# Taking the experts of a mixture in turn, those with two slots and those with one: places ranked on VectorE, each section's weights found by SyncE in a table

## The chip, the cores and the metric

One Trainium2 chip, one of its cores. The metric is the device time of one execution in microseconds (us); for several executions the median is given. The profile and the trace come from one profiled execution, and its times are counted from the span's start.

## The reference

The trunk has two layers over 512 frames of 1024 columns, all in float32. Each layer is a mixer block (two attentions, gated and merged) and then a feed-forward block, which is dense in layer 0 and a mixture of 8 experts in layer 1. The change concerns the mixture alone:

```python
logits = (h @ w_router).astype(jnp.float32)
top_v, top_i = lax.top_k(logits, TOP_K)          # TOP_K = 2 of N_EXPERTS = 8
top_w = jax.nn.softmax(top_v, axis=-1)
combine = jnp.sum(jax.nn.one_hot(top_i, N_EXPERTS) * top_w[..., None], axis=-2)
out = jnp.zeros_like(h)
for e in range(N_EXPERTS):                       # D_FF_EXPERT = 1408
    out = out + combine[..., e:e + 1] * swiglu(h, w_gate[e], w_up[e], w_down[e])
```

512 frames with two experts each make 1024 pairs, 128 per expert on the average. The sum over the experts does not depend on their order.

## The kernel before

The kernel is written engine by engine, with semaphores by hand; each engine's function is a list of instructions in the order in which it runs them. It has no scheduler. Every float32 product is made of three matmuls of rounded halves (high by high, low by high, high by low), for which ScalarE writes the high half of each weight unit and VectorE the low half.

**Routing.** TensorE computes the router's logits and turns them so that frames lie on partitions. VectorE finds the two largest per frame with small operations on 32 columns, and writes picks. TensorE multiplies picks by a triangle and by ones, which gives each frame's rank within its expert (columns 0 to 31 of bank 3) and the number of frames of each expert (columns 64 to 71). From the ranks VectorE works out a column and a row of the lists for each of the 1024 entries (spot, lines 1061 to 1076), writes them as one-hot tiles (in_column, entry_hit, row_hit, lines 1078 to 1085), and TensorE sums these into lists, which hold for each slot of each expert the frames to fetch and the rows to store to. Nearly each of these operations is wrapped in link(), which makes VectorE wait until it is done. The twice_e tile, written by POOL, is twice the expert's number and so the column of its first slot: place and expert are the same.

**Sections.** Then eight sections follow, one per expert, in a hardware loop on each engine (passes on TensorE, VectorE and ScalarE; weights on SyncE; moves on POOL, unrolled). A slot is a block of up to 128 frames of one expert. An expert with at most 128 frames has one slot; one with more has a second, called the tail, of 64 rows. On TensorE, VectorE and ScalarE the body stands twice, for two slots and for one, and each section reads its count from counts and branches (If counts[i] > 128). With the reference's inputs experts 0, 1, 6 and 7 have more than 128 frames and experts 2, 3, 4 and 5 have not, so the sections come as two, two, one, one, one, one, two, two slots.

**Units.** A section reads 35 units of weights: per gate and up 4 of 512 KB for each of two chunks of columns, 4 of 384 KB for the third, and 11 of 512 KB for the down product. SyncE loads unit after unit into m_raw, a ring of 7 buffers (M_RAW). ScalarE copies each into m_hi and VectorE subtracts into m_lo, rings of 5 (M_SPL), so they run 5 units ahead of TensorE across the section's border. A load waits until m_lo of the unit 7 before it is written (m_lo_ready), since then its buffer is free:

```python
own, following = i % EXPERTS, (i + 1) % EXPERTS
for u in range(M_UNITS):
    sp.wait_ge(m_lo_ready, i * M_UNITS + (first * M_UNITS + u + 1))
    expert_unit(own if u + M_RAW < M_UNITS else following, u + M_RAW)
```

**At a section's start** TensorE goes on with the next section's first units, while ScalarE copies the last result (y_stage, line 812), and behind a two-slot section also the upper half of the tail (m_other, line 815), which VectorE adds into y_stage (line 1157). Then ScalarE splits units 5 to 8, takes the SiLU of the first gate chunk and goes on splitting. In unit 8 TensorE waits for VectorE's product m_act (line 1132) to turn it (turn_act, line 1482).

**Around the sections.** POOL gathers the frames of the section after next from h_dram into xg by an indirect DMA (line 520; the first two sections' frames before the loop), and scatters y_stage to y_dram by another (line 543), once per slot; for an absent second slot it moves two rows that lead nowhere (move(2)). At the end SyncE reads y_dram back (line 402), VectorE combines with the two weights, and the final norm follows. In two places TensorE runs matmuls on zeros while it waits (keep_warm, line 1207): 12 behind the ranks and 24 behind the lists.

## Time and profile before

| | |
|---|---|
| median of 3 executions | 1804.72 us (1804.34 to 1805.02) |
| the profiled execution | 1805.55 us |
| its span | 1803.8 us |
| granted TensorE clock, mean | 0.976 |
| TensorE matmuls | 1642.4 us busy, 91% of the span |
| VectorE, ScalarE, GpSimd busy | 1041.5, 895.9, 100.7 us |
| HBM read, written | 244.70 MB, 9.47 MB |

The sections of the experts fill the span from 1210.9 to 1764.7 us. PE is TensorE, PEld its weight loads, DVE VectorE, ACT ScalarE, POOL GpSimd and SP SyncE; a q behind a name is the engine's sequencer. A matmul's record overlaps the next one, so that start to start and not the duration is its price. The granted clock is 1.00 at 2.4 GHz and 0.50 at 1.2 GHz.

### The profile page before, as it was taken

What the parts mean: (1) busy time and instruction counts of PE and PEld (TensorE: products, weight loads), DVE (VectorE), ACT (ScalarE), POOL (GpSimd) and SP (SyncE); (2) the same over time, 40 slices, a digit from 0 to 9 for tenths busy, and PEclk for the clock granted to TensorE, in tenths of its full rate; (3) what the DMA queues carried; (4) which work ended last, traced back from release to release, by engine and by line L of the source; (5) the groups of instructions that cost most, each with busy time, mean ns of one, the idle gap of its engine ahead of it and who ended that gap; (6) DMA issues with size and microseconds to landing.
All of it is one profiled execution on the core that took longest, in us unless ns stands there. A gap on an engine that the chain in (4) does not pass through costs nothing.

```text
span 1803.8 us, 22794 instructions
## 1 busy us (share of the span) xinstructions
PE 1642.4 (91%) x7732; PEld 1334.7 (74%) x7733; DVE 1041.5 (58%) x1715; ACT 895.9 (50%) x1429; POOL 100.7 (6%) x148
## 2 busy tenths in 40 slices
PE   7999987999999999999998879989998999999991
PEld 5877766777888878868777667748787877788881
DVE  6437775645333333354377756466666788776665
ACT  4446665233232222234466643246566777775653
POOL 1000000000000000010000000030101100110002
PEclk9999999999999999999999999989999999999995
DMA  6432111322333323343321112256767899996674
GB/s 170 127 98 61 50 49 46 93 85 72 101 94 95 104 84 97 99 100 114 100 59 52 57 38 91 66 209 190 240 198 255 325 330 342 338 319 214 209 222 162
DMA packets 79109, 259.47 MB, mean 144 GB/s; under 512 B 12384, under 2 KB 12384, under 8 KB 78512
## 3 DMA queue, kind: packets, MB, share of 16 engines
q1 hardware_dynamic: 71056, 239.16, 40.6%
q0 software_dynamic: 7968, 19.21, 3.9%
q8 instruction: 49, 0.80, 0.2%
q14 instruction: 36, 0.29, 0.1%
HBM read 244.70 MB, written 9.47 MB: 141 GB/s over the span
## 4 chain that ended last, share of the span: by engine, by line
PE 73%; DVE 13%; ACT 7%; issue 4%; DMA 2%; ACTq 0%; DVEq 0%; POOLq 0%; POOL 0%; SPq 0%; PEldq 0%
PE ps L1200 15%; PE ps L1201 15%; PE ps L1202 15%; PE ps L1472 5%; PE ps L1474 5%; PE ps L1473 5%; PE ps L1470 3%; PE ps L1471 3%; DVE w_lo L849 2%; ACT w_hi L574 2%; DVE ps L935 2%; ACT m_hi L761 1%; PE ps L1323 1%; DVE m_lo L1102 1%; DVE y_sum L965 1%
## 5 line engine op out<-in xcount | busy, mean ns | idle before, releaser
L849 DVE TENSOR_TENSOR w_lo<-raw,w_hi 128x1024 fp32r<-128x1024 f32 x166 | 201.3, 1213 | 415.2 <-ACT w_hi L574 415.1
L1200 PE MATMUL ps<-h_hi,w_hi 128*128 128x512 f32 x1008 | 402.5, 399 | 11.9 <-DVE h_lo L992 8.1
L1102 DVE TENSOR_TENSOR m_lo<-m_raw,m_hi 128x1024 fp32r<-128x1024 f32 (+1 forms) x285 | 325.7, 1162 | 134.1 <-ACT m_hi L761 127.9
L1201 PE MATMUL ps<-h_lo,w_hi 128*128 128x512 f32 x1008 | 394.9, 392 | 0.0
L1202 PE MATMUL ps<-h_hi,w_lo 128*128 128x512 f32 x1008 | 394.4, 391 | 0.0
L761 ACT ACTIVATE m_hi<-m_raw 128x1024 fp32r<-128x1024 f32 (+1 forms) x285 | 283.2, 1011 | 173.5 <-PE ps L1471 130.4
L574 ACT ACTIVATE w_hi<-raw 128x1024 fp32r<-128x1024 f32 x166 | 173.9, 1048 | 374.8 <-PE ps L1202 374.8
L1200 PEld LDWEIGHTS ps<-h_hi,w_hi 128*128 128x128 f32 x1008 | 190.3, 189 | 48.1 <-DVE h_lo L992 9.8
L1202 PEld LDWEIGHTS ps<-h_hi,w_lo 128*128 128x128 f32 x1008 | 190.0, 189 | 41.3
L1201 PEld LDWEIGHTS ps<-h_lo,w_hi 128*128 128x128 f32 x1008 | 190.8, 189 | 29.4
L1472 PE MATMUL ps<-m_hi,xt_hi 128*128 128x512 f32 (+1 forms) x384 | 147.2, 383 | 4.6 <-PEq L1486 1.6
L1473 PE MATMUL ps<-m_lo,xt_hi 128*128 128x512 f32 (+1 forms) x384 | 145.0, 378 | 0.0
L1474 PE MATMUL ps<-m_hi,xt_lo 128*128 128x512 f32 (+1 forms) x384 | 145.0, 378 | 0.0
L1472 PEld LDWEIGHTS ps<-m_hi,xt_hi 128*128 128x128 f32 x384 | 73.7, 192 | 18.3 <-DVE m_lo L1102 5.0
L1323 PE MATMUL ps<-ident,probs 128*128 128x128 f32 x272 | 52.7, 280 | 32.5 <-DVE probs L949 32.3
L1474 PEld LDWEIGHTS ps<-m_hi,xt_lo 128*128 128x128 f32 x384 | 73.6, 192 | 10.7
L1473 PEld LDWEIGHTS ps<-m_lo,xt_hi 128*128 128x128 f32 x384 | 73.7, 192 | 10.4
L1323 PEld LDWEIGHTS ps<-ident,probs 128*128 128x128 f32 x272 | 34.6, 140 | 59.8 <-DVE probs L949 50.0
L676 ACT ACTIVATE probs<-ps,stat 128x256 f32<-128x256 f32 (+3 forms) x128 | 61.4, 479 | 33.6 <-DVE stat L935 32.3
L1472 PE MATMUL ps<-m_hi,at_hi 128*128 128x512 f32 x176 | 70.7, 401 | 1.6 <-DVE m_lo L1102 1.6
L1470 PE MATMUL ps<-m_hi,xt_both 128*128 128x512 f32 (+1 forms) x192 | 71.4, 372 | 0.0
L1471 PE MATMUL ps<-m_lo,xt_both 128*128 128x512 f32 (+1 forms) x192 | 71.4, 372 | 0.0
(240 smaller groups left out, 2561.1 us busy)
## 6 DMA issues: line engine op xcount, KB each, us to landing
m_raw<-moe_g SPq DMA_DIRECT2D x135, 512.0 KB, 5.3
m_raw<-moe_down SPq DMA_DIRECT2D x88, 512.0 KB, 5.1
raw<-w_in SPq DMA_DIRECT2D x68, 512.0 KB, 3.5
m_raw<-moe_g SPq DMA_DIRECT2D x64, 384.0 KB, 3.0
raw<-w_gu SPq DMA_DIRECT2D x44, 512.0 KB, 3.5
raw<-w_out SPq DMA_DIRECT2D x16, 512.0 KB, 3.5
raw<-w_down SPq DMA_DIRECT2D x16, 512.0 KB, 3.5
raw<-w_a SPq DMA_DIRECT2D x8, 512.0 KB, 3.5
```

The costliest lines, as they stand in the source:

```text
L574: A.activation(split_of(n, 0, cols)[0], raw[:, n % RAW, 0:cols], ACT.Copy).then_inc(hi_ready, 1)
L761: A.activation(m_hi[:, u % M_SPL, 0:cols], m_raw[:, u % M_RAW, 0:cols], ACT.Copy).then_inc(m_hi_ready, 1)
L849: V.tensor_tensor(lo, raw[:, n % RAW, 0:cols], hi.bitcast(F32), ALU.subtract).then_inc(lo_ready, 1)
L1102: V.tensor_tensor(m_lo[:, u % M_SPL, 0:cols], m_raw[:, u % M_RAW, 0:cols], m_hi[:, u % M_SPL, 0:cols].bitcast(F32), ALU.subtract).then_inc ...
L1200: E.matmul(ps[:, bank, :], wh, hi, start=first, stop=False)
L1201: E.matmul(ps[:, bank, :], wh, lo, start=False, stop=False)
L1202: return E.matmul(ps[:, bank, :], wl, hi, start=False, stop=final)
L1470: E.matmul(out, both[:, x, :], wh, start=start, stop=False)
L1471: return E.matmul(out, both[:, x, :], wl, start=False, stop=stop)
L1472: E.matmul(out, hi[:, x, :], wh, start=start, stop=False)
L1473: E.matmul(out, hi[:, x, :], wl, start=False, stop=False)
L1474: return E.matmul(out, lo[:, x, :], wh, start=False, stop=stop)
```

## The change

Places and experts are no longer the same. The place of a section in the order is worked out on VectorE: two says which experts have over 128 frames, phase which differ in that from expert 0, nth how many experts of the same kind have a smaller number. when = 2 * nth + phase is a different number for each expert, even for the kind of expert 0 and odd for the other, and place is how many experts have a smaller one. Expert 0 is always at place 0. With the reference's inputs the order is 0, 2, 1, 3, 6, 4, 7, 5, and the sections have two, one, two, one, two, one, two and one slot. place2 (twice the place) takes over from twice_e for the column of the lists. Behind row_hit the table is inverted: order holds the expert at each place and by_turn the frames at each place, and counts is taken from by_turn, so that all engines but SyncE follow without a change. SyncE reads two entries of order at the start of each section. For that it has already asked for 12 units of expert 0 before its loop (M_AHEAD = 7 + 5), and in the loop for units 12 and on; each load still waits for the m_lo 7 units before.

```diff
 M_RAW, M_SPL = 7, 5
+M_AHEAD = M_RAW + M_SPL
 M_UNITS = 8 * len(CHUNKS) + KFE
...
         most = sb("most", [P, 1], I32, routed)
+
+        order = sb("order", [P, EXPERTS + 1], I32, routed)
+        pairs = sb("pairs", [P, 3, EXPERTS, EXPERTS], F32, routed)
+        turn = sb("turn", [P, 9, EXPERTS], F32, routed)
         routed.close()
...
 
-            for u in range(M_RAW):
+            for u in range(M_AHEAD):
+                if u >= M_RAW:
+                    sp.wait_ge(m_lo_ready, u - M_RAW + 1)
                 expert_unit(0, u)
 
             def weights(first, sections):
                 with sp.Fori(0, sections) as i:
-                    own, following = i % EXPERTS, (i + 1) % EXPERTS
+                    at = i % EXPERTS
+                    own = sp.value_load(order[0:1, bass.ds(at, 1)], min_val=0, max_val=EXPERTS - 1)
+                    following = sp.value_load(order[0:1, bass.ds(at + 1, 1)], min_val=0, max_val=EXPERTS - 1)
                     for u in range(M_UNITS):
 
-                        sp.wait_ge(m_lo_ready, i * M_UNITS + (first * M_UNITS + u + 1))
-                        expert_unit(own if u + M_RAW < M_UNITS else following, u + M_RAW)
-
+                        sp.wait_ge(m_lo_ready, i * M_UNITS + (first * M_UNITS + u + M_AHEAD - M_RAW + 1))
+                        expert_unit(own if u + M_AHEAD < M_UNITS else following, u + M_AHEAD)
+
+            sp.wait_ge(order_ready, 1)
             weights(0, N_SEC)
...
             one(pool.iota(rt[:, 0, :, :], [[0, TT], [-1, EXPERTS]], base=EXPERTS, channel_multiplier=0,
-                          allow_small_or_imprecise_dtypes=True))
-            one(pool.iota(rt[:, 1, :, :], [[0, TT], [SLOTS, EXPERTS]], base=0, channel_multiplier=0,
                           allow_small_or_imprecise_dtypes=True))
...
             V.wait_ge(route_consts, 1)
-            rank8, twice_e, lg, hit, key, first_, second, rest = (rt[:, j, :, :] for j in range(8))
+            rank8, lg, hit, key, first_, second, rest = (rt[:, j, :, :] for j in (0, 2, 3, 4, 5, 6, 7))
+            lower, same, less = (pairs[:, j, :, :] for j in range(3))
+            tokens, two, phase, nth, when, place, place2, by_turn, number = (turn[:, j, :] for j in range(9))
+
+            def down_(a):
+                return a.unsqueeze(2).to_broadcast([P, EXPERTS, EXPERTS])
+
+            def across(a):
+                return a.unsqueeze(1).to_broadcast([P, EXPERTS, EXPERTS])
+
+            link(V.tensor_tensor(lower, down_(numbers[:, 0:EXPERTS]), across(numbers[:, 0:EXPERTS]), ALU.is_gt))
             both, of_both, of_both_e = rt[:, 5:7, :, :], rt[:, 8:10, :, :], rt[:, 10:12, :, :]
...
             rank, col, row, past1, past2, past3, past4, tails, rounds, col0 = (spot[:, j, :] for j in range(10))
-            link(V.tensor_tensor(of_both_e, both, twice_e.unsqueeze(1).to_broadcast([P, 2, TT, EXPERTS]), ALU.mult))
-            link(V.tensor_reduce(col0, of_both_e, AX.X, ALU.add))
             V.wait_ge(ranks_ready, 1)
 
             ranks = ps[:, 3, 0:TT * EXPERTS].rearrange("p (t e) -> p t e", e=EXPERTS)
+            V.tensor_copy(tokens, ps[:, 3, 64:64 + EXPERTS])
+            V.tensor_scalar(two, ps[:, 3, 64:64 + EXPERTS], float(P), None, ALU.is_gt)
             link(V.tensor_tensor(of_both, both, ranks.unsqueeze(1).to_broadcast([P, 2, TT, EXPERTS]), ALU.mult))
+
+            V.tensor_tensor(same, down_(two), across(two), ALU.is_equal)
+            V.tensor_tensor(phase, two, two[:, 0:1].to_broadcast([P, EXPERTS]), ALU.not_equal)
             link(V.tensor_reduce(rank, of_both, AX.X, ALU.add))
+            V.tensor_tensor(same, same, lower, ALU.mult)
             for at, past in ((P, past1), (CAP, past2), (CAP + P, past3)):
                 V.tensor_scalar(past, rank, float(at), None, ALU.is_ge)
             link(V.tensor_scalar(past4, rank, float(2 * CAP), None, ALU.is_ge))
+            V.tensor_reduce(nth, same, AX.X, ALU.add)
             V.tensor_tensor(tails, past1, past3, ALU.add)
             link(V.tensor_tensor(rounds, past2, past4, ALU.add))
+            link(V.scalar_tensor_tensor(out=when, in0=nth, scalar=2.0, in1=phase, op0=ALU.mult, op1=ALU.add))
+            link(V.tensor_tensor(less, down_(when), across(when), ALU.is_gt))
+            link(V.tensor_reduce(place, less, AX.X, ALU.add))
+            link(V.tensor_scalar(place2, place, float(SLOTS), None, ALU.mult))
+            link(V.tensor_tensor(of_both_e, both, place2.unsqueeze(1).unsqueeze(1).to_broadcast([P, 2, TT, EXPERTS]), ALU.mult))
+            link(V.tensor_reduce(col0, of_both_e, AX.X, ALU.add))
             V.scalar_tensor_tensor(out=col, in0=rounds, scalar=float(SLOTS * EXPERTS - 1), in1=col0, op0=ALU.mult, op1=ALU.add)
...
                                 row[:, mine].unsqueeze(2).to_broadcast([P, TT, P]), ALU.is_equal).then_inc(places_ready, 1)
-            V.tensor_copy(counts[:], ps[:, 3, 64:64 + EXPERTS])
-            link(V.tensor_reduce(most[:], ps[:, 3, 64:64 + EXPERTS], AX.X, ALU.max))
+
+            link(V.tensor_tensor(same, down_(numbers[:, 0:EXPERTS]), across(place), ALU.is_equal))
+            V.tensor_tensor(less, same, across(numbers[:, 0:EXPERTS]), ALU.mult)
+            link(V.tensor_tensor(same, same, across(tokens), ALU.mult))
+            V.tensor_reduce(number, less, AX.X, ALU.add)
+            link(V.tensor_reduce(by_turn, same, AX.X, ALU.add))
+            V.memset(order[:, EXPERTS:EXPERTS + 1], 0)
+            link(V.tensor_copy(order[:, 0:EXPERTS], number))
+            V.sem_inc(order_ready, 1)
+            V.tensor_copy(counts[:], by_turn)
+            link(V.tensor_reduce(most[:], tokens, AX.X, ALU.max))
             V.sem_inc(counts_ready, 1)
```

VectorE, from the rounds to the column. Before, this follows at once:

```order
L1072 TENSOR_TENSOR spot<-spot 128x8
L1073 SCALAR_TENSOR_TENSOR spot<-spot 128x8 [waits route_step]
L1074 SCALAR_TENSOR_TENSOR spot<-spot 128x8
L1075 TENSOR_TENSOR spot<-spot 128x8 [waits route_step]
L1076 SCALAR_TENSOR_TENSOR spot<-spot 128x8
```

With the change the same place reads (turn holds the tiles of 8 columns, pairs those of 8 x 8, rt of_both_e, spot col0 and col; line 1103 is 1073 of before):

```order
L1096 TENSOR_TENSOR spot<-spot 128x8
L1097 SCALAR_TENSOR_TENSOR turn<-turn 128x8 [waits route_step]
L1098 TENSOR_TENSOR pairs<-turn 128x64 [waits route_step]
L1099 TENSOR_REDUCE turn<-pairs 128x8 [waits route_step]
L1100 TENSOR_SCALAR turn<-turn 128x8 [waits route_step]
L1101 TENSOR_TENSOR rt<-rt,turn 128x64 [waits route_step]
L1102 TENSOR_REDUCE spot<-rt 128x8 [waits route_step]
L1103 SCALAR_TENSOR_TENSOR spot<-spot 128x8 [waits route_step]
```

Six operations stand in between, each waiting for the one ahead of it; the last two came before the ranks until now.

SyncE, before the loop and at the start of its body. Before:

```order
L370 DMA g_row<-g_ffn_row 128x1024 [waits x_updated]
L376 DMA m_raw<-moe_g01 128x1024 x7
L384 UNCONDITIONAL_BRANCH
L384 ISA
L376 ISA [waits m_lo_ready]
L376 DMA m_raw<-moe_g01 128x1024
```

With the change:

```order
L376 DMA g_row<-g_ffn_row 128x1024 [waits x_updated]
L382 DMA m_raw<-moe_g01 128x1024 x7
L382 DMA m_raw<-moe_g01 128x1024 [waits m_lo_ready] x5
L392 UNCONDITIONAL_BRANCH [waits order_ready]
L392 ISA
L394 TENSOR_LOAD order
L394 ISA x2
L395 ISA
L395 TENSOR_LOAD order
L395 ISA x2
L398 ISA
L382 ISA [waits m_lo_ready]
```

Five loads moved from the body to before the loop, and two reads of the table stand at the head of the body.

## Rows read from the trace of the kernel before

**Rows 1.** The chain that ended last, shares by engine, whole span.

```profile
PE 73%; DVE 13%; ACT 7%; issue 4%; DMA 2%; ACTq 0%; DVEq 0%; POOLq 0%; POOL 0%; SPq 0%; PEldq 0%
```

**Rows 2.** Stretches: section 0, 2, 4, sections 2 to 5, sections 6 and 7.

```profile
core 0: us, PE busy (x) PEld busy (x) DVE busy (x) ACT busy (x) POOL busy (x), PEclk, DMA share, GB/s
1210.90:1297.30 86.40, 82.13 (x389) 69.58 (x389) 50.59 (x56) 48.28 (x60) 4.12 (x4) 0.98 0.66 205
1380.70:1437.00 56.30, 52.28 (x239) 43.22 (x237) 44.94 (x47) 43.13 (x49) 5.45 (x4) 0.94 0.86 306
...
1491.30:1544.00 52.70, 49.46 (x239) 41.45 (x238) 44.66 (x46) 42.12 (x48) 5.33 (x4) 1.00 0.94 348
1380.70:1598.20 217.50, 203.73 (x950) 169.83 (x949) 178.87 (x182) 170.00 (x193) 22.39 (x16) 0.97 0.92 332
1598.20:1764.70 166.50, 160.17 (x777) 136.56 (x775) 105.66 (x116) 99.31 (x121) 7.50 (x8) 1.00 0.70 220
```

**Rows 3.** Waits of TensorE from 1298 to 1765: total us, times, longest.

```profile
PE ps L1482 <- DVE m_act L1132: 9.2, 4, 2.9
```

**Rows 4.** Timeline, ScalarE and TensorE, start of section 2 (start us, us).

```profile
1382.91 1.03 ACT L815 ACTIVATE m_other<-ps 64x1024 f32<-64x1024 f32 x1
...
1396.27 1.11 PE L1482 MATMUL ps<-ident,m_act 128*128 128x128 f32 x4 [2.89 <-DVE m_act L1132]
```

**Rows 5.** Timeline, TensorE, start of section 3.

```profile
1451.51 0.65 PE L1482 MATMUL ps<-ident,m_act 128*128 128x128 f32 x4 [2.11 <-DVE m_act L1132]
```

**Rows 6.** Stretches behind these two places (columns as in rows 2).

```profile
1395.50:1402.20 6.70, 5.69 (x15) 4.33 (x16) 3.96 (x6) 1.96 (x3) 0.00 (x0) 0.50 0.83 291
1453.50:1456.80 3.30, 3.30 (x9) 2.54 (x8) 1.89 (x3) 1.06 (x1) 0.00 (x0) 0.50 0.89 318
```

**Rows 7.** Timeline, VectorE and TensorE, routing and the wait for the gather.

```profile
1191.66 0.22 DVE L1066 TENSOR_TENSOR rt<-rt,ps 128x64 f32<-128x64 f32 x1 [0.21 <-PE ps L1435]
1191.92 0.22 DVE L1067 TENSOR_REDUCE spot<-rt 128x8 f32<-128x64 f32 x1
...
1192.60 0.17 DVE L1071 TENSOR_TENSOR spot<-spot 128x8 f32<-128x8 f32 x1
1192.68 0.16 DVE L1072 TENSOR_TENSOR spot<-spot 128x8 f32<-128x8 f32 x1
1192.88 0.17 DVE L1073 SCALAR_TENSOR_TENSOR spot<-spot 128x8 f32<-128x8 f32 x1
...
1197.00 0.21 DVE L1091 TENSOR_SCALAR lists<-ps 128x48 uint32<-128x48 f32 x1 [0.59 <-PE ps L1441]
...
1196.80 7.04 PE L1207 MATMUL ps<-idle 128*128 128x512 bf16 x24
...
1207.95 1.97 PE L1453 MATMUL ps<-ident,xg 128*128 128x128 f32 x8 [3.23 <-DMA xg<-h_dram,lists]
```

**Rows 8.** Landing of m_raw, 1437 to 1492 (min, median, max); ScalarE's waits, 1200 to 1803.

```profile
DMA to landing us min/median/max: 3.1/5.4/7.2
...
ACT m_hi L761 <- DMA m_raw<-moe_down: 0.6, 1, 0.6
...
ACT m_hi L761 <- DMA m_raw<-moe_g: 0.4, 2, 0.2
```

**Rows 9.** SyncE's read of most (ns); timeline of VectorE, section 2.

```profile
L398 SPq TENSOR_LOAD <-most x1: 472/472/472, 1756.3 to 1756.3; - x1
...
1382.01 1.23 DVE L1102 TENSOR_TENSOR m_lo<-m_raw,m_hi 128x1024 fp32r<-128x1024 f32 x1 [1.04 <-ACT m_hi L761]
...
1386.35 4.63 DVE L1102 TENSOR_TENSOR m_lo<-m_raw,m_hi 128x1024 fp32r<-128x1024 f32 x4 [1.16 <-ACT m_hi L761]
```

**Rows 10.** POOL's second scatter, section 4's start and the end; landings, 1764 to 1803, 1437 to 1600.

```profile
1495.71 0.90 POOL L543 DMA_INDIRECT y_dram<-x_rows,lists x1 [0.34 <-issue]
...
1771.00 0.93 POOL L543 DMA_INDIRECT y_dram<-y_stage,lists x1 [2.26 <-issue]
...
DMA to landing us min/median/max: 2.5/2.5/2.5
...
DMA to landing us min/median/max: 6.2/6.5/6.7
```

More of the change, by code:

```diff
@@ L220, in build_kernel @@
         places_ready, lists_summed, lists_ready, counts_ready = sem("places_ready"), sem("lists_summed"), sem("lists_ready"), sem("counts_ready")
+        order_ready = sem("order_ready")
         pool_step = sem("pool_step")
```

## Prediction, made before the changed kernel ran

> **What bounds the kernel now.** I read the chain of waits first, then the expert phase section by section, then the few idle places of TensorE in it. A section is one expert; I number them by their place in the order, 0 to 7. In the chain that ended last TensorE has 73% and no transfer more than a few per cent [rows 1], so a shorter time has to come from fewer or shorter stops of TensorE. The stretches show two kinds of section. With two slots TensorE runs 388 matmuls and a section takes 83.2 us (the last two take 166.5 together); with one slot it runs 238 and takes 52.7 to 56.3 us; the first section takes 86.4 [rows 2]. In both kinds TensorE is busy 93 to 96% of the time, and the reader is to see that the four one-slot sections, which stand in a row, lose no more of it than the others although their DMA share is 0.92 against 0.70. Its largest wait after section 0 is the one for the product tile m_act, 9.2 us in four pieces, one in each one-slot section, up to 2.9 us [rows 3]. That piece is longer in section 2, behind a two-slot section (2.89 us), than in section 3, behind a one-slot section (2.11 us), and the reason stands before it on ScalarE: the copy m_other of 1.03 us, which only a two-slot section leaves behind [rows 4, 5]. After this stop TensorE's granted clock fell to 0.50, its level of 1.2 GHz, for 6.7 us in section 2 and 3.3 us in section 3; section 4, with the same stop as section 3, kept 1.00 [rows 6, 2]. That, and not the weights, makes the one-slot sections differ among themselves.
>
> **The change, part by part.**
>
> Routing. The change puts a ranking of eight places into the chain of small VectorE operations between the counts and the lists. In that chain an operation on 64 columns that the next waits for takes 0.26 us from start to start, one on 8 columns 0.20, and one that nobody waits for at once 0.08 [rows 7]. Before the column of an entry is known there are six new waited-for operations: four on 64 columns (less, place, of_both_e, col0: 4 x 0.26) and two on 8 (when, place2: 2 x 0.20), together 1.44 us, and six not waited for at 0.08 to 0.10, 0.54. That is 2.0 us. The two operations that left the place ahead of the ranks stood in a wait for TensorE and give nothing back. Behind the last row_hit there are five waited-for ones (three on 64 columns, the cast to order and the maximum: 3 x 0.26 + 2 x 0.20 = 1.18) and four others (0.36), 1.54 in all. Two short ones stand there now, 0.23 us together with the 0.16 of the last, and then VectorE is idle for 0.59 until TensorE's sums at 1197.00 [rows 7]; 1.54 - 0.23 - 0.59 leaves 0.7 us that sticks out. The lists, the gather of rows and the first product all wait for this, so routing costs **+2.7 us**. The ranking mask (lower) is hidden: it runs while VectorE waits for the logits. TensorE's 24 idle matmuls (7.0 us) wait for the counts and so start 3.0 us later; they and the first eight transposes (1 us) then end near 1207.9, and the second gather lands near 1210.7, 2.7 after the 1207.95 of now [rows 7]. If they run at half clock they end after it and cost up to 1.8 us more. Bounds: +1.3 (the operations without waiters free, the end hidden) and +4.5.
>
> SyncE. The table is read where 12 units of the section are already asked for. Per section that is two register loads, each 0.47 us by the one such load that SyncE has, with a register operation or two behind it: I count 1.4 us for both [rows 9]. The load of unit 12 waits for the fifth unit's m_lo. In section 2 VectorE finished unit 4 at 1383.2 and unit 5 only near 1387.5, since y_stage, m_other and the load of an activation table stand on ScalarE between their splits, so 4 us cover 1.4 [rows 9, 4]. I take 0. Without that cover the load of unit 12 would come up to 1.4 us late; queued behind the read are only the later weight loads and ScalarE's split waits for them. The distance between a load and the unit that frees its buffer is unchanged (7 buffers).
>
> Weights in turn. This is where a gain could be. In section 3 the m_raw loads land after 5.4 us in the middle and 7.2 at most, and ScalarE's wait for them in the whole phase comes to 0.4 us for moe_g and 0.6 for moe_down [rows 8]. So spreading the demand gives at most 1.0 us, and I take 0. The Trainium skill, DMA: Bandwidth & Descriptors, section Specifications, puts a core's share of HBM at about 358 GB/s. The 348 GB/s of section 4 [rows 2] is 97% of that, so by this rule four one-slot sections in a row have no reserve and the turn-taking should pay. That is the first rival below.
>
> One-slot sections behind two-slot sections. Now all four are such, before one was. Each gets the longer stop of section 2: 52.7 + 0.8 = 53.5 us at full clock. With a short stretch at half clock (half of 3.3) it is 55.1, with the long one it is section 2 itself, 56.3. I take 55.5, a little nearer to the short one, because a longer stop makes a fall likelier, yet of the stretches seen one was long and one short [rows 6]. 4 x 55.5 = 222.0 against 217.5 [rows 2]: **+4.5 us**. Bounds: 4 x 52.7 = -6.7, and 4 x 56.3 = +7.7. Two-slot sections stay at 83.2 whatever stands before them (section 6 stands behind a one-slot one, section 7 behind a two-slot one). The first section keeps its 86.4.
>
> The end. The last section has one slot, and there are 12 loads past its end instead of 7, of which the last five are issued as it ends. Now POOL's second scatter starts at 1771.0 and lands 2.5 us later [rows 10]. Behind a one-slot section POOL stands 0.34 us before the second, empty scatter instead of 2.26, but such a pair landed 6.2 to 6.7 us after its issue with weight loads beside it [rows 10]. So 1.9 us are won and about 4 lost: **+2.0 us**. Bounds: -1.9 (lands in 2.5) and +2.3.
>
> Sum: 2.7 + 0 + 0 + 4.5 + 2.0 = +9.2 us. The profiled execution took 1805.55, so 1814.8; it stood 0.8 over the median of the runs, which gives **1813.9 us**.
>
> **The rivals.** (1) The queue gets relief, and the kernel becomes faster. Place: the one-slot sections, where TensorE idles 52.7 - 49.5 = 3.2 us. If late weights were behind these stops, three sections would get them back, -9.6, and with routing the sum is -6.9: 1797.8. It decides as soon as ScalarE's waits for m_raw are over the 2.7 us of routing; they are 1.0 at most [rows 8], which speaks against it, while the share of 0.92 speaks for it. The page's limit named above is the same mechanism. (2) The clock holds. One-slot sections take 53.5 and the end costs nothing: 2.7 - 3.5 = -0.8, 1803.9; with the end 1805.9. For it: section 4 kept 1.00. Against it: its stop was the shorter one. (3) The clock falls long in each one-slot section and over the idle matmuls: 4.5 + 7.7 + 2.3 = +14.5, 1819.2. Section 2 is one such case. (4) SyncE's read is not covered and the late loads reach TensorE in the one-slot sections: 4 x 1.4 = 5.6 on top, 1819.5. The 4 us of cover speak against it. (5) It does not do what it says: the order stays in fact as it was. Then only routing stays, 1807.4. The two kinds are four and four now, so a right table must alternate.
>
> **How the numbers follow.** Chances: forecast 0.50 (its own range 1809 to 1818), rival 1 0.08, 2 0.17, 3 0.17, 4 0.05, 5 0.03. The range 1805.5 to 1819.5 takes in rivals 3 to 5 and half of 2, and leaves out rival 1 and the edges. About 0.2% (3.6 us) is what a measurement of this kernel can tell from no change. Below 1801.1 lies rival 1: 0.08. Between, rivals 2 and 5: 0.20. Above 1808.3 the rest: 0.72.
>
> **What would show it.** Sections with 388 and 238 matmuls in turn; lists written 2.7 us later; PE's wait for m_act near 2.9 us in all four one-slot sections, each with a stretch at 0.50 behind it; the four together 219 to 225 us; two-slot ones at 83; the second scatter landing 10 to 11 us after the last product instead of 8.8. The forecast is wrong if one-slot sections come out at or under 53 us, if ScalarE's waits for m_raw had been more than they look, or if SyncE's loads start late and ScalarE waits for them at units 12 and 13.

## The result, and the profile after

| | changed kernel | kernel before, same runs |
|---|---|---|
| median | 1819.95 us (1815.27 to 1824.43, 4 executions) | 1804.87 us (1804.34 to 1806.84, 4 executions) |
| profiled execution, its span | 1815.27, 1813.5 us | 1805.55, 1803.8 us |
| granted clock in it | 0.975 | 0.976 |

The ratio is 1.008, 95% interval 1.0059 to 1.0101: **slower by 0.8%**. The four executions had a mean granted clock of 0.975, 0.969, 0.972 and 0.970, and the faster ones are those with the higher clock. Span times clock, a rough estimate of the time at full clock (the clock is rounded to 0.001, which is 1.8 us), gives 1765 to 1768 us for the four. For the kernel before it gives 1758 to 1763 us, 1761 on the average, over the 14 executions beside runs 1, 2, 5 and 6. So two things are in the result: 5 to 8 us at any clock (5 by these averages, 7 to 8 in the profiled pair), and a clock that is lower on the average.

The profiled execution is 9.72 us over that of the kernel before. Cut at the picks (the last routing operation that both kernels share), the first product of the expert phase and its last product, it splits like this:

| part | before | after | difference |
|---|---|---|---|
| start to the picks | 1190.80 | 1192.28 | +1.5 |
| picks to the first product | 20.1 | 22.0 | +1.9 |
| the four one-slot sections | 217.5 | 221.0 | +3.5 |
| the four two-slot sections | 336.3 | 335.7 | -0.6 |
| last product to the end | 39.1 | 42.5 | +3.4 |

The first part holds nothing of the change but the small operation for the mask lower. It differs by the stretches at half clock, which the profiles of both kernels show there in different places. In the profiled executions of this kernel, of the kernel before and of the eleven runs below it took 1188.1 to 1192.3 us, so single executions differ by 4 us ahead of the change.

The chain of waits of the changed kernel, answering to [rows 1]; the new name in it is SPq:

```profile
PE 73%; DVE 13%; ACT 7%; issue 4%; DMA 2%; SPq 1%; ACTq 0%; DVEq 0%; POOL 0%; POOLq 0%; PEldq 0%
```

Routing in the changed kernel, timeline of VectorE and then of TensorE (start us, busy us, engine, line, operation), answering to [rows 7]:

```profile
1192.28 0.19 DVE L1077 TENSOR_TENSOR picks<-rt 128x32 bf16<-128x32 f32 x1
...
1199.63 0.22 DVE L1117 TENSOR_TENSOR pairs<-numbers,turn 128x64 f32<-128x64 f32 x1
...
1201.38 0.21 DVE L1130 TENSOR_SCALAR lists<-ps 128x48 uint32<-128x48 f32 x1 [0.16 <-DVE most L1126]
...
1194.83 0.81 PE L1246 MATMUL ps<-idle 128*128 128x512 bf16 x3
1198.70 2.15 PE L1480 MATMUL ps<-entry_hit,row_hit 128*128 128x96 f32 x8 [3.06 <-DVE row_hit L1114]
1201.34 7.50 PE L1246 MATMUL ps<-idle 128*128 128x512 bf16 x24 [0.48 <-DVEq L1127]
...
1211.88 1.39 PE L1492 MATMUL ps<-ident,xg 128*128 128x128 f32 x8 [2.18 <-DMA xg<-h_dram,lists]
```

From the picks to the lists it is 9.10 us where it was 6.20: the ranking costs 2.9 us. TensorE now stands 3.06 us before the sums that make the lists. What waits in the end is the second gather, and one microsecond of the 2.9 is caught up there and in the transposes, which ran at a better clock than before (1.39 us instead of 1.97). Over all profiles, the first product came 21.3 to 23.3 us after the picks in the seven kernels with the ranking (22.4 on the average) and 19.7 to 20.1 us in the six without (19.9): the ranking delays it by 2.5 us.

The sections of the changed kernel, as stretches between their last products, answering to [rows 2]; they hold 238 and 389 products in turn, so the order is what the change says:

```profile
core 0: us, PE busy (x) PEld busy (x) DVE busy (x) ACT busy (x) POOL busy (x), PEclk, DMA share, GB/s
...
1300.10:1357.00 56.90, 51.29 (x238) 42.70 (x238) 45.13 (x47) 43.55 (x49) 5.32 (x4) 0.97 0.88 307
1357.00:1440.30 83.30, 80.14 (x389) 68.39 (x388) 52.72 (x58) 49.16 (x60) 4.45 (x4) 1.00 0.71 237
1440.30:1494.00 53.70, 49.63 (x238) 41.34 (x237) 44.89 (x47) 43.11 (x49) 6.26 (x4) 1.00 0.90 322
...
1577.30:1632.60 55.30, 51.26 (x238) 42.48 (x237) 44.94 (x47) 43.10 (x49) 6.37 (x4) 0.97 0.89 317
...
1715.90:1771.00 55.10, 51.04 (x238) 42.13 (x236) 44.92 (x47) 43.11 (x49) 4.48 (x4) 0.97 0.87 312
```

Two stops make the one-slot sections long. The first line below is the wait list of TensorE in this phase (total us, times, longest), answering to [rows 3]; then its timeline at the border behind the first section and in the first three one-slot sections, answering to [rows 4, 5]:

```profile
PE ps L1521 <- DVE m_act L1171: 10.1, 4, 2.9
...
1299.88 0.39 PE L1510 MATMUL ps<-m_lo,at_both 128*128 128x512 f32 x1
1303.35 0.49 PE L1511 MATMUL ps<-m_hi,xt_hi 128*128 128x512 f32 x1 [3.08 <-DVE m_lo L1141]
...
1318.93 0.66 PE L1521 MATMUL ps<-ident,m_act 128*128 128x128 f32 x4 [1.42 <-DVE m_act L1171]
1455.88 0.65 PE L1521 MATMUL ps<-ident,m_act 128*128 128x128 f32 x4 [2.92 <-DVE m_act L1171]
1592.88 0.65 PE L1521 MATMUL ps<-ident,m_act 128*128 128x128 f32 x4 [2.92 <-DVE m_act L1171]
```

The long stop of [rows 4] is there in three sections, 3.3 us from the start of the last product before it to the turning of m_act. Stops are counted in this way, start to start, from here on. The first one-slot section is another case: at its border TensorE stands 3.47 us (1299.88 to 1303.35; 1.45 us at the same border of the kernel before), and its stop for m_act is the shorter for it, 1.8 us. The border in the kernel before:

```profile
1295.82 0.39 PE L1471 MATMUL ps<-m_lo,at_both 128*128 128x512 f32 x1
1297.27 0.49 PE L1472 MATMUL ps<-m_hi,xt_hi 128*128 128x512 f32 x1 [1.06 <-DVE m_lo L1102]
```

Answering to [rows 6] (columns as above), the stretch behind the border stop, those at the stops that end at 1592.88 and 1731.46, and last the one behind the stop that ends at 1455.88:

```profile
1304.70:1308.10 3.40, 3.40 (x10) 2.65 (x9) 0.47 (x1) 2.70 (x3) 0.93 (x1) 0.50 0.69 263
1594.80:1598.20 3.40, 3.40 (x10) 2.63 (x9) 2.01 (x3) 1.06 (x1) 0.00 (x0) 0.50 0.82 287
1731.40:1734.80 3.40, 3.10 (x9) 2.32 (x10) 2.80 (x3) 0.60 (x1) 0.00 (x0) 0.50 0.94 307
1455.00:1465.00 10.00, 8.89 (x40) 7.25 (x41) 8.11 (x10) 6.16 (x8) 0.00 (x0) 1.00 0.78 262
```

Three sections had a short stretch at 0.50 (55.1 to 56.9 us) and one kept 1.00 (53.7).

SyncE's read of the table, durations in ns, minimum, median, maximum, answering to [rows 9]:

```profile
L394 SPq TENSOR_LOAD <-order x8: 271/274/471, 1208.8 to 1719.4; - x8
...
L395 SPq TENSOR_LOAD <-order x8: 263/271/368, 1210.0 to 1720.2; - x8
```

Each takes 0.27 us in the median, where the prediction took 0.47. The list of ScalarE's waits in this phase holds none for a transfer.

The end, answering to [rows 10]: POOL's scatters, the landing of the second (min, median, max us after its issue), and the transfers in flight at the end:

```profile
1773.97 1.02 POOL L552 DMA_INDIRECT y_dram<-y_stage,lists x1 [3.79 <-ACT y_stage L821]
1775.36 0.90 POOL L552 DMA_INDIRECT y_dram<-x_rows,lists x1 [0.36 <-issue]
...
DMA to landing us min/median/max: 7.6/7.6/7.6
...
m_raw<-moe_g SPq DMA_DIRECT2D x3, 512.0 KB
g_row<-g_final_row SPq DMA_DIRECT2D x1, 512.0 KB, 8.3
```

The second scatter is issued 1.9 us earlier after the last product than before and lands 7.6 us later, 12.0 us after the last product instead of 8.8. In front of it and beside it stand the weight loads past the end, the last issued 2.7 us after the last product and landed 9.7 us after it, and behind them the load of g_row, another 512 KB.

### The profile page after: what moved, and what is told of

It reads as the page before. It is cut to its first block, busy times and chain, and to the rows that moved or that the text cites. A ratio compares the mean times of both kernels' runs of the same rounds, so it can differ in the third digit from the quotient of the medians.

```text
span 1813.5 us, 22881 instructions
## 1 busy us (share of the span) xinstructions
PE 1644.6 (91%) x7732; PEld 1335.9 (74%) x7733; DVE 1044.8 (58%) x1733; ACT 895.7 (49%) x1429; POOL 100.6 (6%) x147
## 4 chain that ended last, share of the span: by engine, by line
PE 73%; DVE 13%; ACT 7%; issue 4%; DMA 2%; SPq 1%; ACTq 0%; DVEq 0%; POOL 0%; POOLq 0%; PEldq 0%
PE ps L1239 15%; PE ps L1240 15%; PE ps L1241 15%; PE ps L1511 5%; PE ps L1513 5%; PE ps L1512 5%; PE ps L1509 3%; PE ps L1510 3%; DVE w_lo L858 2%; ACT w_hi L583 2%; DVE ps L944 2%; PE ps L1362 1%; DVE y_sum L974 1%; DVE m_lo L1141 1%; ACT m_hi L770 1%
## 5 line engine op out<-in xcount | busy, mean ns | idle before, releaser
L1239 PE MATMUL ps<-a_hi,w_hi 128*128 128x512 f32 x176 | 69.4, 394 | 3.1 <-DVE act L1023 3.1
```

Of the source, the lines that this page charges most:

```text
L1239: E.matmul(ps[:, bank, :], wh, hi, start=first, stop=False)
```

## The experiments

All ratios are to the kernel before on the same chip, with the 95% interval. A kernel of constant order has its table written at the start and no ranking, copies the counts one by one, and loads 12 units past the end, as the change does.

**1. The ranking with the old order.** Everything of the change stays, but a place is the expert's number.

```diff
-link(V.scalar_tensor_tensor(out=when, in0=nth, scalar=2.0, in1=phase, op0=ALU.mult, op1=ALU.add))
+link(V.scalar_tensor_tensor(out=when, in0=nth, scalar=0.0, in1=numbers[:, 0:EXPERTS], op0=ALU.mult, op1=ALU.add))
```

> The changed kernel with one operand other: `when` becomes the expert's own number, so all the ranking, the table and the 12 loads ahead stay, and the order of the sections is that of before. Theory (routing and the order each cost on their own): lists written some 3.0 us later than before relative to the ranks, sections as before (one-slot sections 52.7 to 56.3, together near 217.5), the end some 0 to 1 us longer, in all +2.5 to +4 us against before, and runs that agree with one another as those of before do. Rival (the table read by SyncE is what costs): the same +9 to +15 us as the changed kernel. Rival (noise of the clock alone): the same spread of the runs, 9 us, as the changed kernel.

Measured: 1813.82 us, ratio 1.0046 (1.0029 to 1.0063). Lists again 9.10 us after the picks, first product 23.1 us after them (20.1 before, 22.0 after). The end takes 41.7 us: although the last section has two slots, 12 loads reach past it. So about half of the loss is there without any alternation. That is more than was expected: 8.3 us by the ratio instead of 2.5 to 4, with an end that is 2.6 us longer instead of 0 to 1.

**2. The alternation without the ranking**, and **3. its control, the old order (0 to 7) in the same form.**

```diff
+ORDER = (0, 2, 1, 3, 6, 4, 7, 5)
...
+for p, e in enumerate(ORDER):
+    pool.memset(rt[:, 1, :, e], float(SLOTS * p))
+    pool.memset(order[:, p:p + 1], e)
```

> The order of the change without its ranking: the places 0, 2, 1, 3, 6, 4, 7, 5 are constants that POOL writes long before, the counts are copied one by one into that order, and SyncE reads the constant table with 12 loads ahead. It therefore serves these inputs alone. Theory: the lists come at the time of before, the sections and the end are those of the changed kernel (the four one-slot sections 219 to 225 us together, the end 3.4 us longer), and the runs spread as widely: +6 to +12 us. Rival (routing is most of the loss): within 3 us of before. Rival (the turns help and only the ranking hid it): faster than before.

> The constant table with the order of before: neither ranking nor turns, only SyncE's table, the 12 loads ahead and eight small copies of the counts. Theory: lists at the time of before, sections as before, the end +2.6 us as in the kernel with the ranking and the same order, in all +2 to +4 us against before; the difference to that kernel (about 3 us more) is the ranking. Rival (the table read or the loads ahead cost in each section): sections longer than 52.7 and 83.3 us at full clock, +6 us or more.

Measured: turns 1815.85 us, ratio 1.0057 (1.0038 to 1.0075); control 1806.97 us, ratio 1.0007 (0.9997 to 1.0017). The lists come 6.22 us after the picks in both. The difference, 0.0050 or 9 us (give or take 4), is the price of the alternation; that between run 1 and the control, 0.0039 or 7 us (give or take 4), the price of the ranking. With the control's own 0.0007 they add up to 0.0096, over the 0.0080 of the changed kernel but inside its interval. The table and its reads cost nothing that can be measured. In the profiles the end takes 40.3 us with the turns and 41.2 in the control, against 39.1 before, so what it lost is owed to the 12 loads, and not to the kind of the last section. One-slot sections of the turns, then of the control (columns as above):

```profile
1295.90:1353.00 57.10, 51.28 (x239) 42.74 (x239) 45.01 (x47) 43.46 (x49) 5.31 (x4) 0.97 0.87 309
...
1436.30:1491.60 55.30, 51.28 (x239) 42.51 (x238) 44.95 (x47) 43.11 (x49) 5.36 (x4) 0.97 0.90 318
...
1574.90:1631.40 56.50, 52.44 (x239) 43.32 (x238) 44.93 (x47) 43.11 (x49) 6.36 (x4) 0.94 0.86 301
...
1714.70:1771.20 56.50, 52.48 (x238) 43.22 (x236) 44.94 (x47) 43.11 (x49) 4.10 (x4) 0.94 0.86 304
```

```profile
1381.20:1434.90 53.70, 49.66 (x239) 41.37 (x238) 44.96 (x47) 43.12 (x49) 5.13 (x4) 1.00 0.90 316
1434.90:1489.10 54.20, 50.97 (x239) 42.56 (x238) 44.66 (x46) 42.09 (x48) 5.30 (x4) 0.97 0.94 343
1489.10:1543.40 54.30, 50.97 (x239) 42.55 (x238) 44.60 (x46) 42.08 (x48) 5.33 (x4) 0.97 0.93 335
1543.40:1598.50 55.10, 50.85 (x239) 42.43 (x238) 44.74 (x46) 42.53 (x48) 5.31 (x4) 0.97 0.95 340
```

225.4 us against 217.3. The stops are those of the theory, 3.3 us behind a two-slot section and 2.5 behind a one-slot one (but for one of 3.5 in the control's last), and after the same stop the clock fell not at all, short (0.97 over the section) or long (0.94). The first section of the turns holds a border stop of 3.66 us.

**4. Grouped: the four two-slot sections first, then the four one-slot ones.** The table is (0, 1, 6, 7, 2, 3, 4, 5); the end is that of the turns.

> The constant table with the order 0, 1, 6, 7, 2, 3, 4, 5: four two-slot sections, then four one-slot sections; one border from two slots to one instead of four, with the 12 loads ahead and a one-slot section at the end. Theory (each one-slot section behind a two-slot one has a stop of 3.3 instead of 2.5 us, and the first border costs 2 us more where it leads into the one-slot code): the first border's stop 1.5 to 2.2 us, one stop of 3.3 and three of 2.5 us, the four one-slot sections 212 to 219 us, 4 to 8 us less than the constant table in turns. Rival (a run of one-slot sections starves on its weights, as the change supposes): ScalarE waits for m_raw more than 1 us, the last three one-slot sections over 55 us each at full clock.

Measured: 1810.82 us, ratio 1.003 (1.002 to 1.004), under the turns by 5 us (give or take 4). The first two of the four one-slot sections, and the sum of the four:

```profile
1548.50:1603.70 55.20, 51.16 (x239) 42.48 (x238) 44.96 (x47) 43.10 (x49) 5.86 (x4) 0.97 0.90 313
1603.70:1657.90 54.20, 50.97 (x238) 42.55 (x237) 44.57 (x46) 42.08 (x48) 5.30 (x4) 0.97 0.93 338
...
sum 218.10, PE 204.30 PEld 170.03 DVE 178.90 ACT 169.35 POOL 19.57; mean PE 51.08 PEld 42.51 DVE 44.73 ACT 42.34 POOL 4.89
```

In a row, at a DMA share of 0.90 to 0.93, they take 218.1 us; in turn, at 0.86 to 0.90, 225.4. That is the opposite of what relief for the transfers would give. The border stop is shorter too (2.65 us where the turns have 3.66), though over the 1.5 to 2.2 expected. This kernel is still 4 us over the control, which has about the same stops for m_act; its profile shows 0.8 us more at the border and two more stretches of 3.4 us at 0.50, one behind the border and one behind the stop of 3.3 us.

**5. Idle products in the stop of the changed kernel.** TensorE does 12 products of zeros while it would wait for m_act.

```diff
 def turn_act(c):
+    if c == 0 and slots == 1:
+        keep_warm(12)
```

> The changed kernel with 12 matmuls on zeros put before TensorE's wait for m_act in a one-slot section (2.6 us of work in a stop of 3.3 us), whose result nobody reads. Theory (the stop lets the granted clock fall, and how often it does makes both the spread and half the loss): no stretch at 0.50 in the four one-slot sections, each 53.5 to 53.7 us, runs within 3 us of each other, and 3 to 10 us less than the changed kernel's 1820. Rival (the time is lost to the order itself, to SyncE or to the loads): no change beyond 1 us, and the same spread.

Measured: 1811.94 us, ratio 1.0042 (1.0026 to 1.0059), 7 us under the changed kernel by the ratios (give or take 5). The mean granted clock of its four executions is 0.976 to 0.978, where the changed kernel's was 0.969 to 0.975. The stop in its third section and the section:

```profile
1451.81 2.76 PE L1246 MATMUL ps<-idle 128*128 128x512 bf16 x12
1454.84 0.65 PE L1523 MATMUL ps<-ident,m_act 128*128 128x128 f32 x4 [0.27 <-DVE m_act L1171]
...
1439.30:1493.00 53.70, 52.30 (x251) 42.47 (x250) 44.95 (x47) 43.11 (x49) 5.31 (x4) 1.00 0.92 325
```

m_act comes no earlier, so the section is as long as one whose clock held. Three of the four take 53.7; the first has 58.1, with the border stop (3.68 us) and a stretch at 0.50 behind it, which these products don't reach. So what the alternation adds in these three sections at full clock is 1.0 us each (53.7 against the 52.7 of a section behind a one-slot one), 0.8 of it the longer stop, and above that the clock.

**6. The same in the kernel before**, 9 products.

> The kernel before with 9 matmuls on zeros at the same place (1.9 us of work in a stop of 2.5 us). Theory: the two short stretches at 0.50 (3.4 us each, half of it lost) and most of the long one (6.8 us) go away, so -4 to -6 us: 1799 to 1801. Rival (the clock falls for another reason than this stop): within 1 us of before. The matmuls could cost what they add if the stop was shorter: then +1 to +2 us.

Measured: 1800.51 us, ratio 0.9973 (0.9962 to 0.9984): faster than the kernel before. Its four one-slot sections, answering to [rows 2]:

```profile
1381.20:1593.50 212.30, 205.64 (x986) 168.77 (x985) 179.74 (x181) 169.51 (x193) 22.55 (x17) 1.00 0.95 342
```

212.3 us instead of 217.5, at a clock of 1.00 throughout, with a DMA share of 0.95.

**7. The changed kernel with 5 loads past the end** instead of 12.

```diff
-weights(0, N_SEC)
+weights(0, N_SEC - 1)
+last_weights(N_SEC - 1)
...
+    for u in range(M_UNITS):
+        if u + M_AHEAD < M_UNITS + M_SPL:
+            sp.wait_ge(m_lo_ready, i * M_UNITS + (u + M_AHEAD - M_RAW + 1))
+            expert_unit(own if u + M_AHEAD < M_UNITS else 0, u + M_AHEAD)
```

> The changed kernel with 5 instead of 12 loads past the last section's end (ScalarE and VectorE split 5 units past it, the other 7 nobody reads; with more than 192 frames for one expert it would not go on rightly). Theory (the end is longer because the scatter of the last result lands beside weight loads and the row of gains, which before were through): the second scatter lands within 9 us of the last product instead of 12.0, SyncE reads y_dram back some 3 us sooner (at +11.5 to +12.5 instead of +14.9), 2 to 4 us less than the changed kernel, with its spread. Rival (the end is longer because POOL's way to its last semaphore is, or because the last section has one slot): the scatter still lands at +11 to +12, no gain.

Measured: 1812.66 us, ratio 1.0044 (1.0027 to 1.0061), 6.5 us under the changed kernel by the ratios (give or take 5; 2 to 4 expected). In the profile the end takes 37.8 us instead of 42.5. The scatter starts in the same place and lands 5.3 us sooner:

```profile
1775.28 0.90 POOL L560 DMA_INDIRECT y_dram<-x_rows,lists x1 [0.37 <-issue]
...
DMA to landing us min/median/max: 2.3/2.3/2.3
```

The other profiles bear it out: the end takes 40.2 to 42.5 us in the seven kernels with 12 loads past the end, whatever the last section, 39.0 to 39.2 in the three with 7, and 37.0 to 37.9 in the three with 5. Where 12 loads run past a last section of two slots (run 1 and the control) the second scatter landed after 5.0 and 6.0 us, 2.5 in the kernel before.

**8. Both: idle products and the short end.**

> The changed kernel with both repairs, the 12 matmuls on zeros in the stop and 5 loads past the end. Theory (the terms add): 1808 to 1810 us, that is the 1811.9 of the kernel with the matmuls alone less 2 to 4; still 7 to 10 us over the kernel before with its matmuls on zeros (1800.5): routing 2 to 3, the first border 2, three longer stops 2.4. Rival (the turns have a gain of their own that the clock and the end hid): at or under 1803.

Measured: 1807.69 us, ratio 1.0007 (0.9994 to 1.002). The two savings add up (0.0038 and 0.0036). The changed kernel is then as fast as the kernel before; against the kernel before with idle products in the same place it is still 6 us slower. Its ten executions differed by 9.5 us and those of run 6 by 8.2, as much as the four of the changed kernel, so filling the stops for m_act took away time but not the spread (the four executions of run 5 had agreed within 2.6 us).

**9 to 11. Idle products before the sums of the lists.** Between the sums of the picks and those of the lists 24 idle products instead of 12 in the changed kernel (9) and in run 8 (10), 17 instead of 12 in run 6 (11).

```diff
 mm.then_inc(ranks_ready, 1)
-keep_warm(12)
+keep_warm(24)
```

> The changed kernel with 24 instead of 12 idle products between the sums of the picks and the sums that make the lists, where its TensorE stands 3.1 us. Theory: part of the ranking's price is the clock, since the ranked order in the old sequence stood at 1.0046 to the kernel before against 1.0007 of the constant table, 7 us, of which only 3.0 is the later first product. Then the stretch at 0.50 behind that stop goes, the idle products before the gather run at full clock, and the time is 2 to 4 us under the changed kernel's (ratio to the kernel before 1.006). Rival: the first product waits for the gather and not for the idle products, and the clock of this place is worth nothing: ratio 1.008 as before, first product again 22 us after the picks. A second rival: the idle products make the sums of the lists late, lists later than 9.1 us after the picks.

> The changed kernel with idle products in the one-slot sections, with the short end, and with 24 idle products before the lists. Before: 1.0007 without the last. If the clock of that place counts: 0.9985 to 0.9995. If not: 1.0007. What is left over the kernel before with the same idle products (0.9973) is then the ranking's 3 us and the first border's 2 us.

> The kernel before with idle products in its one-slot sections and 17 instead of 12 before the lists, where it stands 1.46 us. If a stop of 1.5 us there already costs clock: 0.996, the fastest of all. If it does not: 0.9973 again, which then stands as a repeat of the run with the idle products in the sections alone.

Measured: (9) 1817.23 us, ratio 1.0056 (1.004 to 1.0071); (10) 1806.74 us, 1.0004 (0.9995 to 1.0013); (11) 1800.94 us, 0.9965 (0.9951 to 0.9979). TensorE's timeline in (9), to be held against the changed kernel's above:

```profile
1197.07 0.65 PE L1480 MATMUL ps<-entry_hit,row_hit 128*128 128x96 f32 x4 [0.47 <-DVE row_hit L1114]
...
1199.70 7.04 PE L1246 MATMUL ps<-idle 128*128 128x512 bf16 x24 [0.92 <-DVEq L1127]
...
1210.28 1.39 PE L1492 MATMUL ps<-ident,xg 128*128 128x128 f32 x8 [2.67 <-DMA xg<-h_dram,lists]
```

The stop of 3 us is filled and the lists come 9.10 us after the picks as before, but the transposes still wait for the gather, and the first product comes 22.05 us after the picks, 22.0 without. At this place itself nothing is won. The median of (9) is 4 us lower, yet the intervals of the two ratios overlap, and (10) and (11) differ from the kernels without the addition by 0.0003 and 0.0008, inside their intervals. The extra idle products are worth nothing that these runs can tell. Run 11 repeats run 6.

## Why the prediction came out as it did

The sign, and the places of the loss, were right: routing, the one-slot sections, the end. The sum fits the profiled execution, +9.2 forecast and +9.7 found, but that is in part luck: 1.5 of the 9.7 lies ahead of the picks, routing and the sections came out 0.8 and 1.6 under their terms there, the end 1.4 over, and it was the fastest of the four. The median, at 1819.95, is 6 us above the 1813.9 forecast and half a microsecond outside the range; the ratio of 1.008 on the 1804.72 that the forecast started from gives 1819.2, just inside.

- **Routing**, +2.7. The lists came 2.9 us later; pricing waited-for operations by their width (0.26 and 0.20 us) held. In the profile 1.9 us of it reached the first product, 3.0 in run 1, 2.5 on the average of all profiles. The 24 idle matmuls took 7.50 us (7.04 before) and did not end later than the gather. By the times of whole executions the ranking costs about 7 us (run 1 against the control, run 3), with an interval of 3 to 11 us. The profiles of these two differ by 5.0 us: 3.4 to the first product, 0.7 ahead of the picks, 0.5 in the sections and 0.5 at the end. Whether the ranking costs anything beyond its own length is not shown; idle products in the stop that it makes did not clearly bring anything back (runs 9 to 11).
- **SyncE**, 0. Right: the reads take 0.27 us, below the 0.47 taken, and the control with table and reads stands at 1.0007.
- **Weights in turn**, 0; rival 1 falls. Run 4 put the four one-slot sections in a row and was faster than the turns, run 6 made them 5 us shorter at a DMA share of 0.95 against 0.92. In the changed kernel's sections ScalarE has no wait for a weight load in its list, in the kernel before 1.0 us in all. A DMA share of 0.92 was thus no sign that the loads held anything up. At the end of the changed kernel, y_in and h_rows come in at over 400 GB/s (the last line of the two below, GB/s in 40 slices from 1770 to 1813); the Trainium skill, DMA: Bandwidth & Descriptors, section Specifications, names about 358 GB/s as a core's limit of HBM. This core runs alone on the chip and is not held to that figure, which rival 1 leaned on.

```profile
DMA  9878999699300004699999999400004704999100
GB/s 305 255 297 305 351 354 267 229 419 393 134 4 0 8 0 69 236 419 434 419 434 419 434 419 434 191 0 0 0 0 194 293 0 175 400 396 423 69 0 0
```

- **One-slot sections behind two-slot sections**, +4.5 from 4 x 55.5 = 222.0. Measured 221.0 in the profiled execution, so +3.5. That execution was a lucky one: from the first to the last product the four kernels with turns and no idle products in the sections (changed kernel, runs 2, 7 and 9) took 556.5 to 563.3 us, 559.8 on the average, and the three of the old order (kernel before, runs 1 and 3) 553.6 to 554.4, 554.0 on the average. So the turns cost 5.8 us in the profiles. The mechanism is shown: in runs 3 and 4 the six stops in sections behind a one-slot one have 2.5 us (one of them 3.5), those behind a two-slot one 3.3, and run 5 takes the clock's part away. Against the text the sections were not alike ("each with a stretch at 0.50"): one kept 1.00. The reading that one-slot sections "lose no more" of TensorE's time than the others was wrong as well: 203.73 of 217.5 us busy are 94%, against 96% of the two-slot ones. The first of the four sections was forecast wrongly. The step that failed here is "The first section keeps its 86.4", which left out its border: where the first section is followed by a one-slot one, TensorE stood 3.5 to 4.7 us there in six kernels (2.9 in run 10), and 1.5 to 2.7 in the six where a two-slot one follows. What TensorE does in that time no run shows. The profile names m_lo in the changed kernel and "issue", that is no releaser at all, in others. That the engine waits for its instructions where the other branch follows would fit, but was not tested.
- **The end**, +2.0. It was +3.4 in the profiled execution. The 1.9 us of an earlier issue were won as said. The size that failed is the landing "6.2 to 6.7 us", taken from the middle of the phase: at the end it was 7.6, and the first scatter needed 8.8. Run 7 shows the cause, the loads past the end.
- **What the sum had no term for.** It was made against one profiled execution, with one draw of the clock after each stop. In the expert phase of all 13 profiles a stretch at 0.50 stands nowhere but at a stop. Of 16 stops of 3.3 us for m_act three were followed by none, six by one of 3.4 us and seven by one of 6.8 us; of ten stops of 2.5 us one by none and nine by one of 3.4 us. The stretch was the long one where the clock fell 0.2 to 0.9 us before the stop was over, and the short one where it fell later than that. So in these profiles a longer stop is not followed by a fall more often, as the prediction had it, but more often by the long one. The kernel before has one stop of 3.3 us in this phase and three of 2.5; the changed one has three of 3.3, the 3.5 us at the border and one of 1.8. (Executions of the kernel before differ too: 14 beside runs 1, 2, 5 and 6 took 1803.2 to 1810.6.)
- **The rest of the gap.** Of the gap of 15.1 us between the medians the averages of the profiles explain 11: 2.5 for the ranking, 5.8 for the turns and 3.1 for the end (42.2 us in the four kernels with the ranking and 12 loads). The other 4 stay open: the three executions without a profile had a lower clock (0.969 to 0.972), and where it was lost no run shows. Rivals 3 (0.17, 1819.2) and 4 (0.05, 1819.5) had the time nearly right. Rival 4 falls with the control, where SyncE's reads cost nothing. Rival 3, the long fall everywhere, named the right mechanism, but no profile shows the long fall in all four sections.

## What to carry to other kernels

In this kernel a stop of TensorE of 2.5 us or more cost its length and then, from one execution to the next, nothing or up to 2.8 us more of products at half speed (56.5 against 53.7 us). So count such stops and don't only sum them, price them from more than one profile, and price an order of work by what each section leaves on the engines for the next one. Products of zeros that end just before the awaited tile are worth a trial where the wait can't be shortened; here they made the kernel before 0.27% faster (0.16 to 0.38), which no change of order did. Prefetches that run past the end of a loop delay the small transfer that the next stage waits for, so cut them off in the last round, and before spreading transfers out ask whether an engine waited for one at all.

## What the runs showed of the hardware

- Stops of TensorE of 3.3 us were followed by a clock of 1.00 (3 of 16 in all profiles), by 3.4 us at 0.50 (6) or by 6.8 us (7), in sections of the same work. Of ten stops of 2.5 us nine were followed by 3.4 us at 0.50, of four of 1.8 us one (run 9), and of the 52 of 2.0 us in the two-slot sections none. None of the 20 stops for m_act with products of zeros in them was (runs 5, 6, 8, 10 and 11).
- The border behind the first section cost TensorE 2.9 to 4.7 us where the next section takes the other branch of the loop's body, and 1.5 to 2.7 us where it takes the same one. No later border, to the same branch or to the other, shows a stop of over 1.2 us. The cause is open.
- The same small scatter landed 2.3 us after its issue where the last weight load had landed before it, and 7.6 us after it where loads of 512 KB were still in flight (run 7 and the changed kernel).
